# Seven block products in place of eight in the last feed-forward layer of a hybrid decoder step

## The reference

```python
D_FF = 4 * D_MODEL

def squared_relu_mlp(h, w1, w2):
    return jnp.square(jax.nn.relu(h @ w1)) @ w2

        h = rmsnorm(x, gl[2])
        x = x + rmsnorm(squared_relu_mlp(h, w_ff1[l], w_ff2[l]), gl[3])
```

## Time and profile before

| | |
|---|---|
| runs | 2659.51 us median of 3 (2658.62 to 2661.24) |
| profiled execution, its own time | 2657.77 us |
| its span | 2656.0 us |
| PE busy | 2582.1 us, 97% |
| DVE busy | 1385.4 us, 52% |
| ACT busy | 1127.5 us, 42% |
| POOL busy | 249.9 us, 9% |
| stage `ff(1, 1)` | from about 2251.8 us to the end |

### The profile page before, as it was taken

The page is one execution under the profiler, slowest core; times in us unless marked ns, Lnnn a source line. Parts: engine busy times, 40 slices in busy tenths (PEclk is TensorE's granted clock), DMA queues, the critical chain, the costliest instruction groups (busy, mean ns, idle before and its releaser), DMA issues.

```text
span 2656.0 us, 39212 instructions
## 1 busy us (share of the span) xinstructions
PE 2582.1 (97%) x16262; PEld 2301.5 (87%) x16262; DVE 1385.4 (52%) x2209; ACT 1127.5 (42%) x1915; POOL 249.9 (9%) x402
## 2 busy tenths in 40 slices
PE   7998989899999999999999999999999999999998
PEld 5778988788787798899999989998877888999998
DVE  4746774656564465534454465535544456444344
ACT  5564446455444244433333345433332344333324
POOL 5121111100101001100000001110000000000000
PEclk8999999999999999999999999999999999999999
DMA  6454335533323345543333245554434334233322
GB/s 188 158 156 114 109 105 142 154 93 94 104 88 100 113 141 161 177 127 100 116 88 105 88 124 156 171 143 130 119 119 144 103 115 127 84 110 110 96 88 82
DMA packets 368721, 321.47 MB, mean 121 GB/s; under 512 B 11929, under 2 KB 339667, under 8 KB 368544
## 3 DMA queue, kind: packets, MB, share of 16 engines
q1 hardware_dynamic: 336224, 207.91, 26.9%
q0 software_dynamic: 32320, 111.05, 13.4%
HBM read 261.33 MB, written 57.58 MB: 120 GB/s over the span
## 4 chain that ended last, share of the span: by engine, by line
PE 83%; DVE 7%; ACT 5%; issue 2%; DMA 1%; POOL 1%; DVEq 0%; ACTq 0%; POOLq 0%
PE dense L591 74%; PE mixer L591 8%; DVE wlo L1627 2%; ACT arena L1116 1%; ACT whi L1116 1%; DVE arena L1849 1%; DMA proj<-ffh 0%; DVE ffh L1666 0%; ACT relu L1116 0%; ACT ffh L1116 0%; DVE hf L1765 0%; DVE arena L1851 0%; ACT L1116 0%; DMA arena<-xrow 0%; DVE hlo L1761 0%
## 5 line engine op out<-in xcount | busy, mean ns | idle before, releaser
L591 PE MATMUL dense<-hhi,whi 128*128 128x272 f32 (+1 forms) x3072 | 850.8, 331 | 29.4 <-DVE wlo L1627 19.0
L591 PE MATMUL dense<-hlo,whi 128*128 128x272 f32 (+1 forms) x3072 | 826.5, 323 | 0.0
L591 PE MATMUL dense<-hhi,wlo 128*128 128x272 f32 (+1 forms) x3072 | 826.4, 323 | 0.0
L1627 DVE TENSOR_TENSOR wlo<-wst,whi 128x1024 fp32r<-128x1024 f32 x384 | 469.4, 1222 | 242.7 <-ACT whi L1116 241.7
L591 PEld LDWEIGHTS dense<-hhi,whi 128*128 128x128 f32 x3072 | 516.6, 189 | 89.4 <-DVE wlo L1627 24.8
L1116 ACT ACTIVATE whi<-wst 128x1024 fp32r<-128x1024 f32 x384 | 403.7, 1051 | 419.9 <-PE dense L591 416.0
L591 PEld LDWEIGHTS dense<-hhi,wlo 128*128 128x128 f32 x3072 | 515.4, 189 | 42.5
L591 PEld LDWEIGHTS dense<-hlo,whi 128*128 128x128 f32 x3072 | 517.8, 189 | 37.4 <-issue 0.7
L591 PE MATMUL dense<-h1hi,whi 128*128 128x272 f32 (+1 forms) x1536 | 422.6, 329 | 12.5 <-DVE wlo L1627 8.1
L591 PE MATMUL dense<-h1hi,wlo 128*128 128x272 f32 (+1 forms) x1536 | 414.3, 324 | 0.0
L591 PE MATMUL dense<-h1lo,whi 128*128 128x272 f32 (+1 forms) x1536 | 412.2, 323 | 0.0
(11 more groups left out here) (348 smaller groups left out, 1808.5 us busy)
## 6 DMA issues: line engine op xcount, KB each, us to landing
wst<-in_w_ff_dram SPq DMA_DIRECT2D x256, 512.0 KB, 4.0
wst<-in_w_in_even_dram SPq DMA_DIRECT2D x48, 512.0 KB, 4.0
wst<-in_w_in_odd_dram SPq DMA_DIRECT2D x48, 512.0 KB, 3.9
proj<-ffh POOLq DMA_DIRECT2D x48, 272.0 KB, 2.4
proj<-ffh POOLq DMA_DIRECT2D x48, 256.0 KB, 2.3
arena<-proj POOLq DMA_DIRECT2D x16, 512.0 KB, 4.7
wst<-in_w_out_even_dram SPq DMA_DIRECT2D x16, 512.0 KB, 3.6
arena<-proj POOLq DMA_DIRECT2D x8, 1024.0 KB, 8.1
```

The costliest lines, as they stand in the source:

```text
L591: return pe.matmul(out, lhsT, rhs, start=start, stop=stop)
L1627: TT(wlo[:, u % 2, :], wst[:, u % 2, :], whi[:, u % 2, :].bitcast(F32), ALU.subtract)\
```

## The change

In blocks 2 to 7 of `ff(1, 1)` two `f1` units with neighbouring k form a pair. The pair's 256 output features and 8 input tiles are a 2 x 2 matrix of weight blocks (`a11`, `a12`, `a21`, `a22`: unit u or u+1, its first or last four tiles, 512 columns each), and the activations `h` are a 2 x 2 matrix of blocks of four tiles by 272 tokens. The 2 x 2 product is computed with seven block products of sums and differences in place of eight plain ones. Each block product `("p", u, n)` is 4 tiles x 3 = 12 matmuls of 128 x 272, so a pair is 84 matmuls in place of 96, in 12 pairs. What the seven need:

- Sums of the activations, once: items `("t", 0)` to `("t", 4)` (`x_sums`) on DVE, 14 subtractions or additions and 4 copies of 128 x 1088, laid into the rows of block 1.
- Sums of the weights, per pair: `weight_sums` on POOL, four instructions of 128 x 512.
- Splits of seven operands of 512 columns per pair in place of two of 1024: 7 `hi` on ACT and 7 `lo` on DVE. They go round a ring of five quarters (`RINGS`); the fifth lies in `hhi0` and `hlo0`, the activations of group 0, which are free by then. The second pair of a block is loaded into `raw2` in `accA`.
- Products 2, 4 and 6 go on adding in the bank of product 0, and 5 in that of 3: each must wait until the one before is read out (`SEVEN_AFTER`). ACT copies out 0 and 3 and applies ReLU to 6; DVE copies out 2 and adds 1, 4 and 5 to the kept ones (128 x 272 each).
- ReLU and the squares of a pair: `first_half` at item 5 for unit u (ReLU and two squares of 128 x 544 on ACT), and in `seventh(u, 6)` for unit u+1.

The side work of norm 14 and the output tiles moves from 240 rows of the stage into its first 40. Three start-up semaphores (`ident_ready`, `ones_ready`, `consts_ready`) become one that counts to 3. The core of the diff:

```diff
+SEVEN = range(2, FG)
+RINGS = ((0, 1, 2, 3, 4, 0, 1), (2, 3, 4, 0, 1, 2, 3))
+SEVEN_READ = ("act", "dve", "dve", "act", "dve", "dve", "act")
+SEVEN_BANK = "XYXZXZX"
+SEVEN_AFTER = {2: 0, 4: 2, 5: 3, 6: 4}
...
         rows = self.ff(1, 1)
-        self.mix(rows[:-16], rest(2) + self.norm(14, False) + [("y", t) for t in range(4)] + rest(12))
+        n = 2 * PIECES[1] * FK * SEVEN[0]
+        self.mix(rows[:n - 24], rest(2) + self.norm(14, False) + [("y", t) for t in range(4)])
+        self.mix(rows[n - 24:n - 12], [("t", 0), ("t", 1)])
+        self.mix(rows[n - 12:n - 3], [("t", 2), ("t", 3), ("t", 4)])
+        self.mix(rows[n - 3:-16], [])
...
+            def seventh(u, n):
+
+                r = PLAN.op[u, n]
+                pe.wait_ge(S("w_split"), r + 1)
+                if PLAN.pair[u] == 0 and n in (2, 3, 4, 6):
+                    pe.wait_ge(S("t_split"), {2: 2, 3: 1, 4: 4, 6: 3}[n])
+                fresh = n not in SEVEN_AFTER
+                if fresh:
+                    begin((u, n))
+                else:
+                    evac_wait(pe, (u, SEVEN_AFTER[n]))
...
+                for t in range(KH):
+                    for i, (w, x) in enumerate(((wh, xh), (wh, xlow), (wl, xh))):
+                        last = pe.matmul(out, w[:, t * P:(t + 1) * P], x[:, t, :], start=fresh and t == 0 and i == 0,
+                                         stop=t == KH - 1 and i == 2, skip_group_check=True)
...
+                if n in (0, 3):
...
+                    A_(keep[:, n // 3, :], out, ACT.Copy).then_inc(S("act_evac"), 1)
+                elif n == 6:
+                    r = relu2[:, (f + 1) % 2]
+                    act.wait_ge(S("h1_split"), f)
+                    A_(r[:, 0:XC], out, ACT.Relu).then_inc(S("act_evac"), 1)
+                    evac_wait(act, (u, 4))
+                    after(own(A_(r[:, XC:2 * XC], r[:, XC:2 * XC], ACT.Relu)))
+                    evac_wait(act, (u, 6))
+                    squares(u + 1)
+
+            def first_half(u):
+
+                r = relu2[:, PLAN.ff1_rank[u] % 2, 0:GN[1]]
+                evac_wait(act, (u, 5))
+                after(own(A_(r, r, ACT.Relu)))
+                squares(u)
...
+            def weight_sums(u):
...
+                if p:
+                    pool.wait_ge(S("w_split"), PLAN.op[next(v for v in PLAN.pair if PLAN.pair[v] == p - 1), 4] + 1)
+                halves = lambda v: (raw(v)[:, 0:KH * P], raw(v)[:, KH * P:2 * KH * P])
+                (a11, a12), (a21, a22) = halves(u), halves(u + 1)
+                add = pool.tensor_tensor
+                step(add(sums[:, 0, :], a11, a21, ALU.subtract))
+                add(sums[:, 1, :], a22, sums[:, 0, :], ALU.subtract).then_inc(S("w_sum"), 1)
+                add(a21, a21, a22, ALU.add).then_inc(S("w_sum"), 1)
+                pool.wait_ge(S("w_split"), PLAN.op[u, 1] + 1)
+                pool.wait_ge(S("w_sum"), 3 * p + 1)
+                add(a12, a12, sums[:, 1, :], ALU.subtract).then_inc(S("w_sum"), 1)
```

More of the change, by code:

```diff
@@ L112, in ff @@
             for k in range(FK):
-                rows += self.unit("f1", l, g, f, k)
+                if not self.seven("f1", l, g, f):
+                    rows += self.unit("f1", l, g, f, k)
+                elif k % 2 == 0:
+                    u = len(self.units)
+                    self.units += [("f1", l, g, f, k), ("f1", l, g, f, k + 1)]
+                    rows += [[("p", u, n)] for n in range(7)]
             for k in range(FK):
@@ L277, in count @@
                 wide = g
+            elif item[0] == "p":
+                u, n = item[1:]
+                key, bank = (u, n), SEVEN_BANK[n]
+                begun_at = {"X": 0, "Y": 1, "Z": 3}[bank]
+                if n == begun_at:
+                    b = min(range(4), key=ended_at)
+                    self.jobs[key] = dict(bank=b, before={last[b]} if b in last else set())
+                    last[b] = (u, {"X": 6, "Y": 1, "Z": 5}[bank])
+                    self.jobs.setdefault(last[b], dict(bank=b))
+                rank += 1
+                reader = SEVEN_READ[n] + "_evac"
+                evac[reader] += 1
+                self.jobs.setdefault(key, {}).update(bank=self.jobs[u, begun_at]["bank"], done=rank,
+                                                     read=(reader, evac[reader]))
+                continue
             elif item[0] in ("on", "gate", "gate2", "misc"):
@@ L1074, in _ @@
                     piece(*item[1:])
+                elif item[0] == "p":
+                    seventh(*item[1:])
                 elif item[0] == "x":
@@ L1218, in unit_end, with squares, seventh @@
                     A_(r, r, ACT.Square).then_inc(S("h1_hi"), 1)
+            def squares(u):
+                f, k = PLAN.ff1_rank[u], PLAN.units[u][4]
+                r = relu2[:, f % 2, 0:GN[1]]
+                after(own(A_(h1hi[:, k, 0:GN[1]], r, ACT.Square)))
+                A_(r, r, ACT.Square).then_inc(S("h1_hi"), 1)
+            def seventh(u, n):
+                f = PLAN.ff1_rank[u]
+                done((u, n))
+                out = DB[:, PLAN.jobs[u, n]["bank"], 0:XC]
+                if n in (0, 3):
+                    if PLAN.pair[u]:
+                        evac_wait(act, (min(v for v in PLAN.pair if PLAN.pair[v] == PLAN.pair[u] - 1), n + 1))
+                    A_(keep[:, n // 3, :], out, ACT.Copy).then_inc(S("act_evac"), 1)
[12 more added lines that the diff above has]
+                squares(u)
             def x_in(t):
@@ L2227, in _ @@
                         unit_begin(item[1])
-                    if item[2] == 1:
-                        lo(item[1] + 1)
+                    for r in PLAN.ahead.get(("d", item[1], item[2] - 1), ()):
+                        lo(r)
                     if item[1] in PLAN.after_conv:
@@ L2233, in _ @@
                         unit_end(key)
+                elif item[0] == "p":
+                    for r in PLAN.ahead[item]:
+                        lo(r)
+                    seventh(*item[1:])
+                elif item[0] == "t":
+                    x_sums(item[1])
                 elif item[0] == "x":
```

204 lines of the change are left out of this document (179 added, 25 removed).

## The result

The changed kernel takes 2684.82 us (median of 5 runs, 2684.41 to 2686.63) against 2660.82 for the kernel before in the same comparison (5 runs, 2658.62 to 2661.82): a ratio of 1.0093, 95% interval 1.0082 to 1.0105. It is slower by 24 us. The forecast was 2684.

The account below looks back on a forecast made before the run. The prediction took TensorE (PE), busy 97% of the span, as the bound: -18.0 us for 144 fewer matmuls, +29.1 for waits in six blocks, +13.2 for the rest, +24.3 in all, so 2684 us; range 2666 to 2696.

Parts of the forecast that it names:

- Term 1: Start of a block's second pair: PE waits for ACT's copy of product 0, +2.9 us, six times; bounds 1.8 and 4.5.
- term 4: Activation sums in block 1: DVE ends late and PE waits, +8 us once; bounds 5.4 and 11.7.
- Term 2: Start of the f2 units: PE waits for DVE's h1lo, +1.35 us, six times.
- Term 3: Small waits inside the pairs, from ACT's late split of product 4 and POOL: +0.6 us, six times; bounds 0 and 1.5.
- Term 5: Side work packed into 40 rows: a few short waits on ACT and DVE, +2 us; bounds 0 and 4.
- Term 6: Lower clock for one stretch after the long wait of term 4: +3.2 us.
- rival B: The clock falls in every block after the waits of term 1: 8.4 us more, 2692 us; chance 0.27.
- A: Rival: POOL does not hold DVE up in the stage, so terms 1, 3 and 4 shrink: 2673 us; chance 0.17.
- C: Rival: the links hide, waits of 0.5 to 1 us per block remain, so the kernel is faster: 2654 us; chance 0.07.

Follow-up runs that it names:

- experiment 5: The kernel before, with only the side work (norm 14, output tiles) in the stage's first 40 rows in place of 240: 2659.86 us, ratio 1.0007.
- experiment 1: The changed kernel with POOL's four weight additions per pair on 16 columns in place of 512, all waits kept: 2673.39 us, ratio 1.0052.
- experiment 4: The changed kernel with DVE adding product 5 of a second pair ahead of the next unit's 1024-column split: 2679.73 us, ratio 1.0076.
- experiment 3: The changed kernel with ACT's copy of product 0 and the split behind it ahead of two squares, in second pairs: 2683.98 us, ratio 1.0093.
- experiment 8: Experiment 6 plus a second buffer for POOL's sums, earlier loads, and activation sums spread over 56 rows: 2649.52 us, ratio 0.9967 to the kernel before.
- experiment 2: The changed kernel with the sums of the activations on 16 columns, their waits kept: 2676.85 us, ratio 1.0065.
- Experiment 6: The changed kernel with ACT's order of experiment 3 and every DVE product evacuation ahead of its item's splits: 2659.4 us, ratio 1.0007.

## Why the prediction held, point by point

**The form of it.** The stage grew by 25.8 us in the profiled runs, and the sum said 24.3. Ledger of the trace: -18.0 for the matmuls, +28.0 of listed waits (30.1 after, 2.1 before), +8.8 for the clock makes +18.8. The other 7.0 are listed as no wait. In block 2414.94 to 2464.84, which has no fall of the clock, I find them so: its 14 products take 24.09 us in place of 21.0 and its f2 part 25.81 in place of 24.40, together 4.5 over; the two listed waits are 3.53 of that, so 1.0 a block lies between matmuls. Six times 1.0 is 5.8 to 6. The last 1 us is unplaced; the stage of experiment 5 is 1.2 us longer than that of the kernel before, with no more in listed waits (2.2), so it may be the denser side work, but one trace of each does not show it.

**Term 1** (2.9 six times) measured 2.29 to 2.30 five times and 1.55 once; with the restart, 2.47 in block 3. It was the step most in doubt and was taken 0.4 to 0.6 too high. Both halves are off the same way: without POOL the wait is 1.5 (experiment 1) where the sum had 1.8, because ACT's ten instructions from the ReLU to the copy took 5.34 us in block 3 where the sum had 5.88 (the recorded durations add to 5.71, and five of them overlap the next by 0.1, which I counted for DVE in term 4 and not here); POOL's share is 0.8 where it had 1.1. The one wait of 1.55 is the block behind the 6.38 us stall: there the last split ahead of the addition took 0.68 (2374.40, POOL idle) and not 1.43.

**Term 2** (1.35 six times): 1.2 listed, 1.4 in block 3. Right, and experiment 4 shows its cause: one split of 1024 ahead of one addition of 0.44.

**Term 3** (0.6): 0.62 in block 3 is what the products take beyond their matmuls and the 2.47, so the size is right, but the reason given is not. The split of product 4 was no longer in the way (done at 2432.2). PE began product 4 behind DVE's copy of product 2, which stood behind another split, as later in experiment 3:

```profile
2433.87 0.43 DVE L1928 COPY accA<-dense 128x272 f32<-128x272 f32 x1
...
2434.45 0.36 PE L791 MATMUL dense<-hhi,whi 128*128 128x272 f32 x1
```

That gap is 0.34 us by the starts of the matmuls. It remains in experiment 8 (0.33), where ACT is no longer behind, so it is not a part of ACT's lateness. The rest is in smaller gaps at the starts of products.

**Term 4** (8): waits of 0.34, 0.70 and 6.38 us, 7.4; taken out it gives 8.0 (experiment 2). The copy of 1088 columns, bounded by 0.7 and 1.29, took 0.73; POOL's part, taken as 2.6, is 2.4 (6.4 less 4.0). DVE's instructions in question, held and not held:

```profile
2354.98 2.26 DVE L1908 TENSOR_TENSOR accA<-accA,hlo 128x1088 f32<-128x1088 f32 x1
2357.27 2.24 DVE L1909 TENSOR_TENSOR accA<-accA,hlo 128x1088 f32<-128x1088 f32 x1
2359.54 0.73 DVE L1911 CAST hhi<-accA 128x1088 fp32r<-128x1088 f32 x1
2360.30 1.29 DVE L1912 TENSOR_TENSOR hlo<-accA,hhi 128x1088 fp32r<-128x1088 f32 x1
```

**Term 5** (2): 1.6 by the medians of experiment 5, within its interval anything from nothing to 4.

**Term 6** (3.2) was the one mis-sized. The stretch behind the long stall came as forecast and cost 2.6. But four more stretches of 3.4 us each at 0.50 followed waits of 2.3 us: 4 x 3.4 x (1 - 0.125/0.23) = 6.2. So rival B, given 0.27, came true in four of six blocks. The total held because two errors cancelled: +5.6 of clock, against 3.4 less in term 1 (17.4 in the sum; 13.0 listed and six restarts of 0.17 in the trace) and 0.6 less in term 4. Which waits appear, where and on whom was forecast; that the sum met 2684 within a microsecond is luck.

**The rivals.** A's mechanism did not apply (means of 907 and 1088 ns, not 690), yet its price was right: experiment 1 made its condition true and gave 2673.39. C assumed waits under 1.2 us a block; they were 3.5. Experiment 6 brought them there by order alone, and 8 took out term 4 too: 8.8 us under the kernel before, where C, with term 4 still in, had 6. (C's sum leaves out the 3.2 of term 6, which its own bound of 1.2 us a block counts; with it C is 2657.) The gain was in the change, and the order in which ACT and DVE worked it off took it.

## What to carry to other kernels

Where a product is accumulated on top of another, its evacuation becomes a link that TensorE waits for: put it ahead of everything else in the queue of the engine that does it, on each engine that has one, before counting what the saved matmuls bring. Price such a change by walking the chain from the last matmul that feeds it to the instruction that frees the bank, summing the engine's own order; a busy share of 40% says nothing about it. And look at each engine of the chain before judging: here ACT's order alone moved the wait to DVE's copy and gained nothing, and both together shortened the stage by 24 us.

## What the runs showed of the hardware

POOL and DVE hold each other on instructions that read only SBUF. In the changed kernel DVE's subtractions of 512 columns took 0.69 us alone and up to 1.80 beside POOL, of 1088 columns 1.29 and 2.26; additions with an input in PSUM stayed at 0.43 to 0.44. The other half, which no row of before showed, is there too: in the second pairs POOL's third sum took 1.74 us on the mean and its fourth, when DVE was mostly done, 1.30 (changed kernel, 2250 to 2684):

```profile
L2849 POOL TENSOR_TENSOR accA<-accA 128x512 f32<-128x512 f32 x6 | 10.4, 1735 | 0.0
...
L2852 POOL TENSOR_TENSOR accA<-accA 128x512 f32<-128x512 f32 x6 | 7.8, 1295 | 4.7 <-DVE wlo L1829 4.7
```

By the Trainium skill (SBUF — State Buffer, "SBUF: two separate sides") whichever of the two starts first keeps the shared port pair for its whole instruction, and the other waits. The trace agrees in both directions: POOL's sum of 2422.93 began while a DVE split ran until 2423.51 and took 0.44 us longer than one alone, and DVE's split of 2423.78 began while that sum ran until 2424.67 and took 0.74 longer.

Waits of TensorE of 2.29 to 2.31 us were followed by 3.4 us at the lower clock (1.2 GHz) four times in five in the changed kernel, six in six in experiment 2 and three in five in experiment 4; behind those of 1.86 to 1.87 us in experiment 3 it fell three times in six, and behind one of 1.53 to 1.55 never (six times in experiment 1, once each in the changed kernel and in experiment 4). Such a stretch costs 1.5 us. The length of the wait alone does not decide it, then; why the same 2.30 us at 2431.08 was not followed by a fall stays open.
